# Adaptive-norm modulation moved from TensorE products to VectorE row sums, and the context's first norm moved into the feed-forward before it

## The chip, the cores and the metric

The kernel runs on one core of one Trainium2 chip. The metric is the device time of one execution in microseconds. Everything is fp32: products that need more than one pass of TensorE's reduced fp32 form are split by hand into a high and a low part (`whi`, `wlo` for weights, `Hhi`, `Hlo` for activations), the high part by a cast on ScalarE, the low part by a subtraction on VectorE.

## The reference, cut to what matters

256 tokens of 1024 features go through a first block (two layers: feed-forward, hybrid mixer, feed-forward) and a second block (two layers over the tokens and a context of 256 tokens). The second block is modulated by two condition vectors:

```python
def adaln(cond, w, b, n_chunks):
    return jnp.split(jax.nn.silu(cond) @ w + b, n_chunks, axis=-1)

# first block: per layer x += 0.5*ffn1(norm x); x += mixer(norm x); x += 0.5*ffn2(norm x); then a final norm
for layer in range(2):
    sh1, sc1, g1, sh2, sc2, g2 = adaln(c, w_mod[layer], b_mod[layer], 6)
    h_lat = rmsnorm(x, norm1_g[layer]) * (1 + sc1) + sh1
    if layer == 1:
        csh1, csc1 = adaln(c_ctx, w_mod[layer][:, :2 * D_MODEL], b_mod[layer][:2 * D_MODEL], 2)
    else:
        csh1, csc1, cg1, csh2, csc2, cg2 = adaln(c_ctx, w_mod[layer], b_mod[layer], 6)
    h_ctx = rmsnorm(ctx, norm1_g[layer]) * (1 + csc1) + csh1
    ...
```

`w_mod` is 2 x 1024 x 6144: 96 tiles of 512 KB. The result for one condition vector is 2 x 6144 numbers, 96 columns of 128 partitions (`MOD`, whose last index is 0 for c and 1 for c_ctx).

## The kernel before, in words

Each engine runs its own list of instructions, written out by hand; the order within an engine is the order of the code, and semaphores join the engines. The stages follow each other: for each layer l of the first block `("ffn1", l)`, `("in", l)` and `("out", l)` (the mixer), `("ffn2", l)`; then `c0` and `x0` (mixer of the second block's layer 0 on the context and on the tokens), `ffc` and `ffx` (its feed-forwards), `ctx_keys_values`, `x1`, and then the routed experts, which take the last 780 us and are not touched.

All weights but `w_mod` are one stream of 512 KB units through a ring of RAW = 11 buffers (`raw`), issued by SyncE. For a unit ScalarE writes `whi` (ring of SPLIT = 6), VectorE writes `wlo`, TensorE uses both and counts `weight_used`. `upto(n)` on ScalarE and VectorE stands for the casts up to unit n.

A feed-forward has NF = 22 steps f: a gate unit, an up unit and, two steps later, a down unit of 24 matmuls. On VectorE (`hidden`) a step is: wait for the gate unit, sum its halves into `gs`, one cast, the low part `hlo` of the step before, wait for the up unit, sum into `us`, multiply into `hd`, two casts. Behind the last step stand the residual adds (`ffn`). Small side jobs are put between: in both `ffn2` the 17 steps of the Hyena filter (`filter_step`; tables by GpSimd's `filter_tables`), in `ffn1` of layer 0 the turning of the context (`first_step`), in `ffc` and `ffx` the norm of the next stage's input (`side_step`).

A norm squares eight tiles (ScalarE), sums them over partitions with a matrix of ones (TensorE), takes sqrt (ScalarE) and reciprocal (VectorE), and then scales tile after tile: VectorE `TT`, ScalarE `HB` high, VectorE `HB` low.

The modulation has six groups of 16 tiles (three for each layer; a tile is 128 rows of `w_mod` by 1024 columns). SyncE loads them between weight units (`mods`) into up to 13 slots. `modulate` multiplies each with `CS`, silu of both condition vectors in 2 of 32 columns, on TensorE: 8 k by 4 column blocks, each a product of 512 columns. `rows_out` (ScalarE) copies the sums out of PSUM to `MR`, `turn_rows` (TensorE) transposes them, `take_rows` (VectorE) adds the bias into `MOD`. Groups 0, 1, 2 and 3 stand around norms (the first two k in front, the other six behind), group 4 in `ffc` at f = 13 and f = 20, group 5 in `ffx` at f = 13 and behind the norm in `ctx_keys_values`.

Behind `("ffn2", 1)` come the final norm of X, the scales `GS`, the norm of the context C with its modulation, and then c0's linear. GpSimd's `fold` adds eight tiles of squares to one, for norms that run beside other work; TensorE then needs one product only (`side_sum`).

## Time and profile before

| | |
|---|---|
| median of 3 runs | 3023.56 us (3022.86 to 3027.97) |
| the profiled execution | 3024.66 us, its span 3022.8 us |
| TensorE, VectorE, ScalarE, GpSimd busy | 2935.2, 2213.8, 1721.4, 75.3 us |
| instructions | 50779 |
| DMA | 692.13 MB, mean 229 GB/s |

Busy time of TensorE is near its span because matmuls are pipelined; where it waits is read from the chain of waits and from the idle time in brackets. In a timeline a row gives the start, the time, the engine, the line, the operation with its tiles, the number of instructions merged into it, and in brackets the idle time of the engine in front of it and what ended that. The tile names `M`, `scratch` and `gscratch` are shared buffers: `COND`, `gs`, `us` and `MR` lie in `M`.

### The profile page before, as it was taken

Reading aid. Unit: us, or ns where it says so; the run is one execution under the profiler, and the core shown is the slowest. Engines: PE = TensorE matmul, PEld = TensorE weight load, DVE = VectorE, ACT = ScalarE, POOL = GpSimd, SP = SyncE. Lnnn points to the kernel's source line nnn. Section 1 sums busy time; section 2 is a strip of 40 time slices with the busy share of each in tenths; the row PEclk is TensorE's granted clock in tenths of the full one; section 3 lists DMA queues with packets and bytes.
Section 4 is the critical chain, followed back from the end, with each engine's and each line's share of the span. In section 5 each row is a group of like instructions: output and inputs, shape, how many; then the busy total and the mean of one; then the engine's idle time right before and its main releaser. Section 6 shows DMA issues by size and latency. Waiting matters only on the chain.

```text
span 3022.8 us, 50779 instructions
## 1 busy us (share of the span) xinstructions
PE 2935.2 (97%) x18783; PEld 2569.6 (85%) x18783; DVE 2213.8 (73%) x2982; ACT 1721.4 (57%) x2379; POOL 75.3 (2%) x103
## 2 busy tenths in 40 slices
PE   9999999999999999999999999999989999999998
PEld 7989788899887889788889888997978888888887
DVE  6667666666677666566676767765678999999998
ACT  4446553444655445445544444455468788878886
POOL 2000000000000000000000000000000000000000
PEclk9999999999999999999999999999999999999999
DMA  8854465886536593465386775735559999999999
GB/s 253 274 181 140 128 189 182 259 274 186 161 119 177 161 282 102 140 175 162 86 253 186 223 238 180 230 105 151 174 197 362 364 354 362 367 361 359 364 363 335
DMA packets 664465, 692.13 MB, mean 229 GB/s; under 512 B 22830, under 2 KB 518145, under 8 KB 663008
## 3 DMA queue, kind: packets, MB, share of 16 engines
q1 hardware_dynamic: 658432, 665.06, 68.4%
q0 software_dynamic: 5712, 24.54, 2.2%
q8 instruction: 124, 2.03, 0.3%
q14 instruction: 53, 0.43, 0.0%
q10 hardware_dynamic: 144, 0.07, 0.0%
HBM read 684.86 MB, written 4.72 MB: 228 GB/s over the span
## 4 chain that ended last, share of the span: by engine, by line
PE 88%; DVE 6%; ACT 3%; issue 2%; DMA 1%; DVEq 0%; POOL 0%; ACTq 0%
PE W L694 35%; PE ACC L694 20%; PE W L787 15%; PE W L788 8%; PE W L687 4%; PE ACC L687 3%; DVE wlo L1885 1%; ACT whi L1393 1%; PE ACC L1001 1%; PE W L1211 1%; PE ACC L1202 0%; DVE R L1904 0%; DVE TT L1911 0%; DVE gs L1973 0%; DVE M L2038 0%
## 5 line engine op out<-in xcount | busy, mean ns | idle before, releaser
L1885 DVE TENSOR_TENSOR wlo<-raw,whi 128x1024 fp32r<-128x1024 f32 (+3 forms) x681 | 765.7, 1144 | 357.9 <-ACT whi L1393 355.8
L1393 ACT ACTIVATE whi<-raw 128x1024 fp32r<-128x1024 f32 (+3 forms) x681 | 655.6, 985 | 48.5 <-PE W L694 31.7
L2394 DVE TENSOR_TENSOR wlo<-raw,whi 128x1024 fp32r<-128x1024 f32 x528 | 617.7, 1221 | 43.3 <-ACT whi L1751 34.3
L787 PE MATMUL W<-HB,whi 128*128 128x512 f32 x1760 | 635.2, 403 | 12.6 <-DVE HB L1907 11.9
L1751 ACT ACTIVATE whi<-raw 128x1024 fp32r<-128x1024 f32 x528 | 547.5, 1060 | 94.7 <-PE W L694 52.7
L788 PE MATMUL W<-HB,wlo 128*128 128x256 f32 x1760 | 496.6, 282 | 0.0
L694 PE MATMUL W<-HB,whi 128*128 128x256 f32 x2592 | 480.2, 287 | 14.0 <-DVE HB L1907 8.1
L694 PE MATMUL W<-whi,HB 128*128 128x512 f32 (+1 forms) x1664 | 478.7, 373 | 4.9 <-issue 3.5
L694 PEld LDWEIGHTS W<-HB,whi 128*128 128x128 f32 x2592 | 407.4, 193 | 22.8 <-issue 12.7
L787 PEld LDWEIGHTS W<-HB,whi 128*128 128x128 f32 x1760 | 333.0, 189 | 102.7 <-issue 17.2
L1465 ACT ACTIVATE sg<-gs 128x256 f32<-128x256 f32 x132 | 55.1, 418 | 593.1 <-DVE gs L1973 593.1
L694 PE MATMUL W<-HB,wlo 128*128 128x256 f32 x1296 | 368.4, 284 | 0.0
L694 PEld LDWEIGHTS W<-whi,HB 128*128 128x128 f32 x1664 | 300.2, 189 | 60.3 <-DVE wlo L2394 4.4
L788 PEld LDWEIGHTS W<-HB,wlo 128*128 128x128 f32 x1760 | 335.6, 191 | 0.0
L694 PE MATMUL W<-wlo,HB 128*128 128x512 f32 (+1 forms) x832 | 307.8, 370 | 0.0
L694 PE MATMUL ACC<-hhi,whi 128*128 128x256 f32 x1056 | 303.9, 288 | 0.0
L694 PE MATMUL ACC<-hlo,whi 128*128 128x256 f32 x1056 | 298.9, 283 | 0.0
L694 PE MATMUL ACC<-hhi,wlo 128*128 128x256 f32 x1056 | 298.8, 283 | 0.0
L694 PEld LDWEIGHTS W<-HB,wlo 128*128 128x128 f32 x1296 | 250.6, 193 | 0.0
L1973 DVE TENSOR_REDUCE gs<-W 128x256 f32<-128x512 f32 x132 | 91.1, 690 | 164.1 <-PE W L788 164.0
L694 PEld LDWEIGHTS ACC<-hhi,whi 128*128 128x128 f32 x1056 | 200.6, 190 | 10.3 <-issue 4.8
L694 PEld LDWEIGHTS ACC<-hlo,whi 128*128 128x128 f32 x1056 | 200.8, 190 | 2.4 <-issue 2.4
(462 smaller groups left out, 4047.2 us busy)
## 6 DMA issues: line engine op xcount, KB each, us to landing
raw<-in_moe_w_gate SPq DMA_DIRECT2D x183, 512.0 KB, 5.3
raw<-in_moe_w_up SPq DMA_DIRECT2D x180, 512.0 KB, 5.4
raw<-in_ffn_w_in SPq DMA_DIRECT2D x176, 512.0 KB, 3.9
raw<-in_moe_w_down SPq DMA_DIRECT2D x176, 512.0 KB, 5.5
raw<-in_w_in SPq DMA_DIRECT2D x105, 512.0 KB, 4.8
raw<-in_ffn_w_out SPq DMA_DIRECT2D x88, 512.0 KB, 3.6
scratch<-in_w_mod SPq DMA_DIRECT2D x60, 512.0 KB, 7.3
raw<-in_mix_w_in SPq DMA_DIRECT2D x48, 512.0 KB, 3.7
```

The source lines that it names most:

```text
L687: return mm(o, a, b, start=start, stop=stop, skip_group_check=True)
L694: last = mm(o, a, b, start=start and i == 0, stop=stop and i == 2, skip_group_check=True)
L787: mm(o, wh[:, w], both(k), start=k == 0, stop=False, skip_group_check=True)
L788: last = mm(o[:, 0:T], wl[:, w], high[:, k, :], start=False, stop=k == KT - 1, skip_group_check=True)
L1001: last = nc.tensor.transpose(bank(4 + b % 2)[:, w], P2[:, (4 * i + b) % 3, w], ident[:, :])
L1211: last = nc.tensor.transpose(W[:, 2 * (g % 2), at], hdt[:, g % 2, at], ident[:, :])
L1393: A_(whi[:, g % SPLIT, 0:LONG[g]], raw[:, g % RAW, 0:LONG[g]], ACT.Copy).then_inc(weight_high, 1)
L1465: A_(sg[:, f % 2, 0:T], gs[:, f % 2, 0:T], ACT.Silu).then_inc(gated, 1)
L1751: A_(whi[:, g % SPLIT, :], raw[:, g % RAW, :], ACT.Copy).then_inc(weight_high, 1)
L1885: V.tensor_tensor(wlo[:, g % RAW, 0:LONG[g]], raw[:, g % RAW, 0:LONG[g]], whi[:, g % SPLIT, 0:LONG[g]].bitcast(F32), ALU.subtract).then_in ...
L1973: return V.tensor_reduce(o, W[:, b, :].rearrange("p (i t) -> p t i", i=2), AX.X, ALU.add)
L2394: V.tensor_tensor(wlo[:, g % RAW, :], raw[:, g % RAW, :], whi[:, g % SPLIT, :].bitcast(F32), ALU.subtract).then_inc(weight_split, 1)
```

## The change

The weights of the modulation come transposed from the host: row n of `w_mod_laid[l]` is column n of `w_mod[l]`, so a tile of 128 outputs by 1024 inputs is 512 KB in one piece. Both condition vectors are broadcast to all partitions (`COND`, silu on ScalarE). One instruction on VectorE multiplies a tile by a condition vector and writes the sum of each row into a column of `MOD`. There are 96 tiles; the first 64 are used for both vectors, the other 32 for c alone: 160 instructions. `MOD_STEPS` says at which step f of which feed-forward a tile is used: 18 in `("ffn1", 0)`, 7 in `("ffn2", 0)`, 22 in `("ffn1", 1)`, 6 in `("ffn2", 1)`, 21 in `ffc`, 22 in `ffx`; in both `ffn2` they stand at steps 2, 10, 12 and so on. GpSimd issues the loads (`mod_tiles`; three slots, one slot in both `ffn2`), and `condition` loads the vectors anew four times, since their buffer is used otherwise between. `modulate`, `turn_rows`, `rows_out`, `take_rows` and `mods` are gone.

The second part: the norm of C for c0 is made in `("ffn2", 1)`. ScalarE squares at f = 13 and 14, GpSimd folds, TensorE sums at f = 18, ScalarE takes sqrt at f = 19, VectorE scales tiles 0 to 3 at f = 20 and 21, the rest and the low parts behind the last step and in front of the residual adds. The final norm of X is now made in c0's linear: squares on ScalarE in front of it, a fold on GpSimd, one sum on TensorE in front of unit 4, sqrt at unit 4, reciprocal at unit 5 and the scaling of a tile in each of units 5 to 12.

The diff, cut to its core:

```diff
+        COND = M[:, 2048:4096].rearrange("p (i k) -> p i k", i=2)
+        JUNK = M[:, 5120:6144]
+
+        def mod_slot(name, i):
+
+            s = 0 if name in FILTERS else i % 3
+            if s == 0:
+                return s, M[:, 4096:5120]
+            return s, (G if name[0] == "ffn1" else S)[:, s * 1024:(s + 1) * 1024]
+
+        def mod_load(name, i):
+
+            u = MOD_FIRST[name] + i
+            return sum(mod_slot(n, j)[0] == mod_slot(name, i)[0] and MOD_FIRST[n] + j <= u
+                       for n in MOD_STEPS for j in range(len(MOD_STEPS[n])))
 
...
+        MOD_STEPS = {("ffn1", 0): range(4, 22), ("ffn2", 0): (2, 10, 12, 14, 16, 18, 20), ("ffn1", 1): range(0, 22),
+                     ("ffn2", 1): (2, 10, 12, 14, 16, 18), "ffc": range(1, 22), "ffx": range(0, 22)}
+        MOD_FIRST, at = {}, 0
+        for name, steps in MOD_STEPS.items():
+            MOD_FIRST[name] = at
+            at += len(steps)
+        assert at == 96
+        COND_AT = {("ffn1", 0): 3, ("ffn2", 0): 2, ("ffn2", 1): 2, "ffc": 1}
+        SIDE = {("ffn2", 1): 0, "x0": 1, "ffc": 2, "ffx": 3}
+        SIDE_INPUT = ("ffc", "ffx")
...
+            def keep_filter(l):
                 pool.wait_ge(freq_taken, 5 * l + 5)
                 pool.dma_start(kept[l], S[:, 2816:5376]).then_inc(kept_out, 16)
-
-            def fold(e, o):
-
-                pool.wait_ge(side_squares, KT * e + KT)
+                pool.wait_ge(kept_out, 16 * l + 16)
+
+            def condition():
+                for i, v in enumerate((A["c_2"][0], A["c_ctx_2"])):
+                    pool.dma_start(COND[:, i, :], v.partition_broadcast(128)).then_inc(cond_in, 16)
+
+            def mod_tiles(name, first, last):
+                for i in range(first, last):
+                    s, dst = mod_slot(name, i)
+                    u = MOD_FIRST[name] + i
+                    if i >= (1 if name in FILTERS else 3):
+                        pool.wait_ge(mod_used, u if name in FILTERS else u - 2)
+                    elif i == 0 and u:
+                        pool.wait_ge(mod_used, u)
+                    if name == ("ffn1", 1) and i == 1:
+                        pool.wait_ge(weight_used, start[name] + 1)
+                    pool.dma_start(dst, A["w_mod_laid"][u // 48, u % 48 * 128:u % 48 * 128 + 128, :]).then_inc(mod_landed[s], 16)
...
+                if l == 0:
+                    condition()
+                mod_tiles(("ffn1", l), 0, len(MOD_STEPS["ffn1", l]))
                 filter_tables(("ffn2", l), l)
+                condition()
+                mod_tiles(("ffn2", l), 0, 5)
+                if l == 1:
+                    fold(flat, side_squares, KT, side_folded)
+                mod_tiles(("ffn2", l), 5, len(MOD_STEPS["ffn2", l]))
+                keep_filter(l)
+            fold(flat, last_squared, KT, last_folded)
             for inst, l, full in MIXES:
...
-            def modulate(group, k0, k1, o):
-                for k in range(k0, k1):
-                    for c in range(2):
-                        u = 16 * group + 2 * k + c
-                        pe.wait_ge(mod_landed[u % 16 % ring(group)], 16 * mod_loads(u))
-                    for j in range(4):
-                        w = mod_slot(16 * group + 2 * k + j // 2)[:, j % 2 * 512:j % 2 * 512 + 512]
-                        last = f32(o[32 * j:32 * j + 32, :], CS[:, k, :], w, k == 0, k == KT - 1)
-                    last.then_inc(mod_used, 2)
...
+                    if name == ("ffn2", 1) and kind == "up" and f == 18:
+                        pe.wait_ge(freq_taken, 10)
+                        side_sum(SIDE[name], W[:, 3, 0:T])
...
-            modulate(3, 0, 2, W[:, 3, :])
-            norm()
-            modulate(3, 2, KT, W[:, 3, :])
+            pe.wait_ge(side_root, 1)
             mix2("c0")
...
+            def early_step(f):
+
+                if f in (13, 14):
+                    for k in range(4 * (f - 13), 4 * (f - 12)):
+                        A_(TT[:, k, :], C[:, k, :], ACT.Square).then_inc(side_squares, 1)
+                if f == 19:
+                    act.wait_ge(side_sums, 1)
+                    A_(R[:, :], W[:, 3, 0:T], ACT.Sqrt, bias=epsc, scale=1.0 / D).then_inc(side_root, 1)
 
...
+                    if COND_AT.get(name) == f:
+                        act.wait_ge(cond_in, 32 * list(COND_AT).index(name) + 32)
+                        A_(COND[:, :, :], COND[:, :, :], ACT.Silu).then_inc(cond_ready, 1)
...
+            def mod_part(name, f, i):
+
+                if f not in MOD_STEPS[name]:
+                    return
+                j = MOD_STEPS[name].index(f)
+                u = MOD_FIRST[name] + j
+                both = u < 64
+                if i == 0 and not both:
+                    return
+                s, w = mod_slot(name, j)
+                if i == 0 or not both:
+                    dve.wait_ge(mod_landed[s], 16 * mod_load(name, j))
+                    if u:
+                        dve.wait_ge(mod_used, u)
+                    if j == 0 and name in COND_AT:
+                        dve.wait_ge(cond_ready, list(COND_AT).index(name) + 1)
+                st = i if both else 0
+                ins = V.scalar_tensor_tensor(w if i else JUNK, w, 1.0, COND[:, st, :], ALU.mult, ALU.mult,
+                                             accum_out=MOD[:, u // 48, u % 48, st:st + 1])
+                if i == 1:
+                    ins.then_inc(mod_used, 1)
+
+            def add_bias(l, t0, t1, both):
+
+                n = 2 if both else 1
+                dve.wait_ge(mod_used, 48 * l + t1)
+                link(V.tensor_tensor(MOD[:, l, t0:t1, 0:n], MOD[:, l, t0:t1, 0:n],
+                                     PV[:, 2, 48 * l + t0:48 * l + t1].unsqueeze(2).broadcast_to([128, t1 - t0, n]), ALU.add))
 
             def first_step(f):
...
+            def early_step(f):
+
+                if f == 4:
+                    add_bias(0, 0, 48, True)
+                    for w in range(2):
+                        scales(0, w)
+                if f == 20:
+                    dve.wait_ge(side_root, 1)
+                    link(V.reciprocal(R[:, :], R[:, :]))
+                if f in (20, 21):
+                    for k in range(2 * (f - 20), 2 * (f - 19)):
+                        side_scale(0, k)
+
...
+                    if f < NF - 1:
+                        mod_part(name, f, 0)
                 low(NF - 1)
+                for i in range(2):
+                    mod_part(name, NF - 1, i)
+                if name == ("ffn2", 1):
+                    for k in range(4, KT):
+                        side_scale(SIDE[name], k)
+                    for k in range(KT):
+                        side_low(SIDE[name], k)
...
```

Three places in the order of instructions. VectorE, two steps' length of `("ffn1", 1)`, before (`gs` and `us` are the sums of the gate and the up unit, `wlo` the casts):

```order
L1885 TENSOR_TENSOR wlo<-raw,whi 128x1024 x2
L1973 TENSOR_REDUCE gs<-W 128x256
L1885 TENSOR_TENSOR wlo<-raw,whi 128x1024
L1977 TENSOR_TENSOR hlo<-hd,hhi 128x256
L1973 TENSOR_REDUCE us<-W 128x256
L2000 TENSOR_TENSOR hd<-sg,us 128x256
L1885 TENSOR_TENSOR wlo<-raw,whi 128x1024 x2
L1973 TENSOR_REDUCE gs<-W 128x256
```

The same place after; the form that writes `MOD` is the multiplication with row sums:

```order
L1893 TENSOR_TENSOR wlo<-raw,whi 128x1024 x2
L1947 SCALAR_TENSOR_TENSOR M,MOD<-gscratch,M 128x1024
L2021 TENSOR_REDUCE gs<-W 128x256
L1947 SCALAR_TENSOR_TENSOR gscratch,MOD<-gscratch,M 128x1024
L1893 TENSOR_TENSOR wlo<-raw,whi 128x1024
L2025 TENSOR_TENSOR hlo<-hd,hhi 128x256
L2021 TENSOR_REDUCE us<-W 128x256
L2049 TENSOR_TENSOR hd<-sg,us 128x256
L1893 TENSOR_TENSOR wlo<-raw,whi 128x1024 x2
L1947 SCALAR_TENSOR_TENSOR M,MOD<-gscratch,M 128x1024
```

One multiplication has moved in front of the gate sum and one behind it. VectorE at the end of `("ffn2", 1)` and the beginning of c0, before (`C` is the context, `X` the tokens; the last cast of c0's first units is at the end):

```order
L1977 TENSOR_TENSOR hlo<-hd,hhi 128x256
L1973 TENSOR_REDUCE us<-W 128x256
L2000 TENSOR_TENSOR hd<-sg,us 128x256
L1885 TENSOR_TENSOR wlo<-raw,whi 128x1024 x2
L1977 TENSOR_TENSOR hlo<-hd,hhi 128x256
L1885 TENSOR_TENSOR wlo<-raw,whi 128x1024
L2017 SCALAR_TENSOR_TENSOR X<-ACC,X 128x256 x8
L1885 TENSOR_TENSOR wlo<-raw,whi 128x1024
L1904 RECIPROCAL R<-R 128x256
L1911 SCALAR_TENSOR_TENSOR X<-X,PV,R 128x256 x8
L1871 MEMSET small 1x1
L2456 SCALAR_TENSOR_TENSOR GS<-MOD,PV 128x8 x2
```

And after:

```order
L2021 TENSOR_REDUCE us<-W 128x256
L2049 TENSOR_TENSOR hd<-sg,us 128x256
L1893 TENSOR_TENSOR wlo<-raw,whi 128x1024 x2
L2025 TENSOR_TENSOR hlo<-hd,hhi 128x256
L1982 SCALAR_TENSOR_TENSOR TT<-C,GS,R 128x256 x4
L1988 SCALAR_TENSOR_TENSOR HB<-TT,MOD,HB 128x256 x8
L1893 TENSOR_TENSOR wlo<-raw,whi 128x1024
L2075 SCALAR_TENSOR_TENSOR X<-ACC,X 128x256 x8
L1893 TENSOR_TENSOR wlo<-raw,whi 128x1024 x6
L2325 RECIPROCAL TT<-TT 128x256
L2327 SCALAR_TENSOR_TENSOR X<-X,PV,TT 128x256
```

The scaling of C and its low parts (`HB`) now stand in front of a cast and of the residual adds (`X<-ACC,X`); the norm of X is behind six casts. TensorE at the same place, before (the products with `CS` are the modulation, those with `ones` the norms):

```order
L694 MATMUL ACC<-hhi,wlo 128x256
L687 MATMUL W<-scratch,CS 32x512 x8
L687 MATMUL W<-TT,ones 128x256 x8
L687 MATMUL W<-scratch,CS 32x512 x4
L687 MATMUL W<-M,CS 32x512 x6
L687 MATMUL W<-gscratch,CS 32x512 x8
L687 MATMUL W<-scratch,CS 32x512 x6
L687 MATMUL W<-TT,ones 128x256 x8
L694 MATMUL W<-HB,whi 128x256 x2
L694 MATMUL W<-HB,wlo 128x256
```

After:

```order
L720 MATMUL ACC<-hhi,whi 128x256
L720 MATMUL ACC<-hlo,whi 128x256
L720 MATMUL ACC<-hhi,wlo 128x256
L720 MATMUL W<-HB,whi 128x256 x2
L720 MATMUL W<-HB,wlo 128x256
L720 MATMUL W<-HB,whi 128x256 x2
L720 MATMUL W<-HB,wlo 128x256
```

Between the last down unit (`ACC`) and c0's first unit (`W<-HB`) nothing is left.

## Rows read from the trace of the kernel before

**Rows 1.** Page, busy time of each engine and share of the span:

```profile
PE 2935.2 (97%) x18783; PEld 2569.6 (85%) x18783; DVE 2213.8 (73%) x2982; ACT 1721.4 (57%) x2379; POOL 75.3 (2%) x103
```

**Rows 2.** Page, chain of waits that ended last, by engine:

```profile
PE 88%; DVE 6%; ACT 3%; issue 2%; DMA 1%; DVEq 0%; POOL 0%; ACTq 0%
```

**Rows 3.** Groups of instructions by form, TensorE: count, busy us, mean ns, idle before:

```profile
L687 PE MATMUL W<-scratch,CS 128*32 128x512 f32 x240 | 32.9, 597 | 1.8 <-DMA scratch<-in_w_mod 1.8
```

**Rows 4.** Chain of waits in order of time: start us, us, what:

```profile
1121.68 5.52 PE W L687 x32
...
1134.26 3.73 PE W L687 x16
...
1150.94 0.44 PE ACC L750 x4
...
1687.67 3.57 PE W L687 x32
```

**Rows 5.** Timeline of VectorE in a step of ffn1, layer 1:

```profile
708.93 2.35 DVE L1885 TENSOR_TENSOR wlo<-raw,whi 128x1024 fp32r<-128x1024 f32 x2
712.79 0.69 DVE L1973 TENSOR_REDUCE gs<-W 128x256 f32<-128x512 f32 x1 [1.50 <-PE W L788]
714.91 1.23 DVE L1885 TENSOR_TENSOR wlo<-raw,whi 128x1024 fp32r<-128x1024 f32 x1 [1.43 <-ACT whi L1393]
```

**Rows 6.** Groups of instructions by form, VectorE:

```profile
L1907 DVE SCALAR_TENSOR_TENSOR HB<-TT,HB 128x256 fp32r<-128x256 f32 x48 | 20.1, 420 | 2.5 <-ACT HB L1423 2.5
L2044 DVE SCALAR_TENSOR_TENSOR scratch<-scratch 128x1536 f32<-128x1536 f32 x4 | 7.0, 1750 | 0.0
L2394 DVE TENSOR_TENSOR wlo<-raw,whi 128x1024 fp32r<-128x1024 f32 x528 | 617.7, 1221 | 43.3 <-ACT whi L1751 34.3
```

**Rows 7.** Timelines of VectorE, TensorE, ScalarE behind ffn1, layer 0:

```profile
210.34 2.91 DVE L2017 SCALAR_TENSOR_TENSOR X<-ACC,X 128x256 f32<-128x256 f32 x8 [0.82 <-PE ACC L694]
212.39 1.92 PE L687 MATMUL W<-scratch,CS 128*32 128x512 f32 x16
214.67 1.28 ACT L1417 ACT_TABLE_LOAD   x1
218.00 0.47 ACT L1417 ACTIVATE R<-W,small 128x256 f32<-128x256 f32 x1 [2.05 <-PE W L687]
```

**Rows 8.** Timelines of VectorE and ScalarE around the beginning of c0:

```profile
1117.19 0.42 DVE L1977 TENSOR_TENSOR hlo<-hd,hhi 128x256 fp32r<-128x256 f32 x1
1119.56 2.92 DVE L2017 SCALAR_TENSOR_TENSOR X<-ACC,X 128x256 f32<-128x256 f32 x8 [0.81 <-PE ACC L694]
1154.29 0.38 ACT L1652 ACTIVATE M<-W 128x256 f32<-128x256 f32 x1 [1.98 <-PE W L694]
```

**Rows 9.** Two norms: a window (TensorE busy, its load, VectorE, ScalarE, GpSimd, clock), timelines:

```profile
356.00:358.00 2.00, 0.70 (x2) 0.56 (x3) 1.82 (x6) 1.33 (x3) 0.00 (x0) 0.50 0.00 0
361.78 0.42 DVE L1907 SCALAR_TENSOR_TENSOR HB<-TT,HB 128x256 fp32r<-128x256 f32 x1 [0.24 <-ACT HB L1423]
365.84 0.69 DVE L1973 TENSOR_REDUCE us<-W 128x256 f32<-128x512 f32 x1 [1.28 <-PE W L788]
580.63 0.43 DVE L1907 SCALAR_TENSOR_TENSOR HB<-TT,HB 128x256 fp32r<-128x256 f32 x1 [0.24 <-ACT HB L1423]
584.54 0.69 DVE L1973 TENSOR_REDUCE us<-W 128x256 f32<-128x512 f32 x1 [0.65 <-PE W L788]
```

**Rows 10.** GpSimd's issue of a table, its landing, ScalarE behind it, a wide form:

```profile
368.01 0.60 POOL L634 DMA_DIRECT2D scratch<-in_k_dft  x1
379.34 0.42 ACT L1590 ACTIVATE scratch<-gscratch 64x256 f32<-64x256 f32 x1 [2.79 <-DVE gscratch L2148]
scratch<-in_k_dft POOLq DMA_DIRECT2D x5, 1408.0 KB, 10.0
L1659 ACT ACTIVATE TT<-M 128x1280 f32<-128x1280 f32 x3 | 3.8, 1273 | 0.6 <-ACTq L1382 0.4
```

**Rows 11.** Timeline of GpSimd, a fold in ffx:

```profile
1840.61 5.15 POOL L642 TENSOR_TENSOR TT<-TT 128x1024 f32<-128x1024 f32 x3 [190.76 <-ACT TT L1443]
```

More of the change, by code:

```diff
@@ L39 @@
 ITEMS = 2 * NE
+WARM = 18
 RAW = 11
@@ L695, in mm3, with linear @@
                 return last
-            def linear(p, units, x, to, by_tile=None, group=None, off=0, free=None, ahead=None, drain=True):
+            def linear(p, units, x, to, by_tile=None, off=0, free=None, ahead=None, drain=True):
                 N = len(units)
                 for n, (kt, nn) in enumerate(units):
-                    if group is not None and n == 2:
-                        turn_rows(group, ACC4[:, 0, :])
                     if ahead is not None:
@@ L763, in ffn @@
                         pe.wait_ge(dve_to_pe, heard.next("dve_to_pe"))
-                    if group is not None and n == 3:
-                        turn_rows(group, W[:, 3, :])
                     pe.wait_ge(weight_split, p + n + 1)
@@ L1801, in _ @@
                 ffn(("ffn2", l))
-            norm(X, after="tiles", ahead=start["c0in"] + AHEAD)
             mix2("c0", 0)
@@ L1941, in first_step, with scales @@
                     V.tensor_scalar(negR[:, :], mask[:, :], 1.0, 2.0 ** 100, ALU.subtract, ALU.mult)
[L1943 removed]
+            SIDES = ((C, 0, 1, 0, 0, Hhi, Hlo), (C, 24, 1, 0, 1, Ghi, Glo), (X, 24, 0, 0, 1, Hhi, Hlo),
+                     (C, 0, 1, 1, 0, Ghi, Glo))
+            def scales(l, w):
+                for st in range(1 if l and w else 2):
+                    V.scalar_tensor_tensor(GS[:, l, st, w, :], MOD[:, l, 8 + 24 * w:16 + 24 * w, st], 1.0,
+                                           PV[:, 3, 16 * w + 8 * l:16 * w + 8 * l + 8], ALU.add, ALU.mult)
+                settle()
             def side_scale(e, k):
@@ L2010, in summed, with ffn @@
                     dve.wait_ge(weight_used, start[name] + sizes[name])
-            def ffn(name, gate, res, group=None, tiles=True):
-                hidden(name, group)
+            def ffn(name, gate, res, tiles=True):
+                hidden(name)
                 for n in range(KT):
@@ L2452, in _ @@
                 ffn(("ffn2", l), lambda n: 0.5, X)
-            def scales(l, w):
-                for st in range(2):
-                    V.scalar_tensor_tensor(GS[:, l, st, w, :], MOD[:, l, 8 + 24 * w:16 + 24 * w, st], 1.0,
-                                           PV[:, 3, 16 * w + 8 * l:16 * w + 8 * l + 8], ALU.add, ALU.mult)
-                settle()
-            norm(X, lambda k: PV[:, 3, 74 + k:75 + k], to=X, told=True, ahead=start["c0in"] + AHEAD)
-            for w in range(2):
-                scales(0, w)
             mix2("c0", 0)
```

223 lines of the change are left out of this document (93 added, 130 removed).

## The prediction

> **What bounds the kernel now.** I read the busy shares first [rows 1]: TensorE is busy for 97% of the span, VectorE for 73%. Then the chain of waits [rows 2]: 88% of it is TensorE's own work. So anything taken off TensorE's queue in a stretch where it never waits is worth its full length, and anything put on VectorE is free only while it fits into that engine's own idle time. Then I asked for the groups of instructions [rows 3]: the modulation's products are 384 matmul records (one of its three groups of rows is shown; 192 products, two records each), with a stationary operand of 32 columns. Last the chain in order of time, at each place where they stand [rows 4].
>
> **Part A, products inside ffc and ffx.** There the chain of waits holds three blocks of 32 records with 3.57 us each [rows 4] (one is shown, the others begin at 1751 and 1883 us). TensorE runs without a pause around them, so they go in full: 3 x 3.57 = 10.7 us. The fourth such block stands behind the norm in front of x1, where TensorE waits for VectorE's normalised tiles anyway: 0.
>
> **Part B, the turns.** Six groups of four transposes; one takes 0.44 us [rows 4]. The one in c0 is counted in part D; five are left, 5 x 0.44 = 2.2 us.
>
> **Part C, products around three norms** (ffn1 to mix of both layers, ffn2 of layer 0 to ffn1 of layer 1). The first two k of a group stand in front of the norm's matmuls and take 1.9 us [rows 7]; the other six stand behind them, where TensorE waits for sqrt, reciprocal and tiles, and cost nothing. What is late next: ScalarE's table load ends at 215.95 (214.67 + 1.28) and its sqrt starts at 218.00, so 2.05 us are to be had there [rows 7]. Behind ffn2 of layer 0 nothing new stands at the end of the steps: 1.9 us. Behind both ffn1, VectorE has two new multiplications before its last cast and the residual adds. The adds, which began at 210.34 after a pause, begin some 1.6 us later, the squares and the table load move with them, and only some 0.5 us of the 2.05 is left. Against it, TensorE now idles where the products stood, and its clock falls: in front of ffn2 of layer 0, a norm without products, it is granted 0.50 (the 1.2 GHz level), and from the last tile (361.78) to the sum of the second unit (365.84) are 4.06 us; in front of ffn1 of layer 1, with products, it is 3.91 us (580.63 to 584.54) [rows 9]. That is 0.15 us, three times 0.5. Part C: 1.9 + 0.5 + 0.5 - 0.5 = 2.4 us.
>
> **Part D, the context's first norm.** Before, the last down unit of ffn2 ends at 1121.68, where the norm's 32 records start [rows 4]; then come X's norm, C's squares and norm (1134.26), the scaling, and c0's third unit ends at 1154.29, where ScalarE is released [rows 8]: 32.6 us. After, the scaled context is ready when ffn2 ends. VectorE's last hlo starts at 1117.19; four scalings (0.40 each), eight low parts (0.40) and one cast (1.2) end at about 1123.5; TensorE needs tile k at 1121.7 + 0.36k, and the last low part is done at about 1122.3, in time for the eighth tile. So three units of 24 matmuls (2.88 each) end 8.6 us after ffn2: 24.0 us less. Added on TensorE: one sum in ffn2 and one in c0, 0.43 each (half of a two-tile stretch at 0.22 a record). Residual adds move from 1119.56 [rows 8] to 1123.5, X's squares end at 1127, GpSimd's fold takes 5.15 us [rows 11] and ends at about 1132.1; TensorE reaches its sum in front of unit 4 at 1133.2. ScalarE's cast for unit 4 is done at about 1128. The cover is 1 us for the fold and 4 us for the cast. Part D: 24.0 - 0.9 = 23.1 us.
>
> **Part E, what VectorE gets.** 160 multiplications over 128x1024. The trace has none with a row sum. Nearest rows [rows 6]: a scalar_tensor_tensor over 256 columns takes 420 ns, over 1536 columns from SBUF 1750 ns, a tensor_tensor over 1024 columns 1221 ns. They lie on one line (about 150 ns + 1.04 ns a column), so 1.22 us without the sum; with it I take 1.3. The bounds are 1.22 and two passes over the tile, 150 + 2 x 1070 = 2.29 us. In a step of ffn1 VectorE has two pauses: 1.50 us before the gate sum, released by TensorE, and 1.43 us before the next cast, released by ScalarE [rows 5]. The order shows one multiplication at each place. At 1.3 both fit, by 0.2 and 0.1 us, so the 40 steps with a pair in ffn1 and the 11 in ffc cost 0; steps of ffx have one. At 1.47 they still fit on the average; beyond, each step is late by twice the excess. The Trainium skill (VectorE: DVE Perf Modes, "Two Vector instructions with no wait between them") says that an operation with an accumulator output is two instructions, the second a read of the accumulator. No row here shows one; that rule would make the 1.22 somewhat longer, as in my 1.3.
>
> **Part F, new waits for transfers.** In each ffn2 ScalarE now waits at f = 2, behind its sine, for c and c_ctx (1 MB), which GpSimd's queue issues right behind the table k_dft. That table is issued at 368.01 and takes 10.0 us for 1408 KB [rows 10]; 1024 KB more at that rate land at about 385. ScalarE is there at 379.7; the silu over 2048 columns takes some 2.0 us (1273 ns for 1280 columns [rows 10]). Behind the waiting ScalarE stand two casts, then VectorE's casts, its multiplication and the next gate sum; casts run 387 instead of 380. TensorE has about four units (11 us) of split weights left, so the first burst is just covered; the next step has 4.5 us of filter work on ScalarE (abs, table load, two exp) and there I count 2 us of pause. Two such places: -4 us, with bounds 0 (all covered) and -16 (both casts of two steps late in full). In ffn1 of layer 0 and in ffc the same silu stands at f = 3 and f = 1 beside idle ScalarE: 0. Weight tiles of the modulation were 96 x 512 KB before and are as many now, only from GpSimd's queue: 0.
>
> **Sum.** 10.7 + 2.2 + 2.4 + 23.1 + 0 - 4 = 34.4 us. The profiled execution took 3024.66 (span 3022.8 and 1.9 around it), 1.1 above the median of 3023.56. 3024.66 - 34.4 = 2990.3, and 2989.2 by the median; I say 2989.
>
> **Rivals.**
> R1, slower: the row sum makes the multiplication take two passes. Place: VectorE's queue in both ffn1. It decides from 1.47 us on. At 2.29 a pair costs 4.58 against 2.93 of pauses, 1.65 a step; 40 steps are 66 us, which show in full because the residual adds stand behind them in the same queue. In ffc 11 x 1.65 = 18, of which later steps with one multiplication give back 6 and TensorE's lead covers some: 10. 2989 + 76 = 3065. Against it: the rows without a sum run at one column a beat whether inputs come from SBUF or not [rows 6]. The Trainium skill (Vector Engine (DVE) Microarchitecture Reference, "Points that are easy to get wrong") says that this form with two sources in SBUF that aren't bf16 halves its throughput, with no port left for the accumulator's readback. By that rule the 1536-column row would be near 3.3 us if it held for every such instruction; it is 1.75, so without a sum the trace contradicts it, and with one no row decides.
> R2: the hand-over to c0 is late, since VectorE's queue at the end of ffn2 (scalings, low parts, cast, adds) slips by 3 us and the fold behind it too: TensorE waits for tiles and again before unit 4, some 12 us of the 23 go. 3001. For it: the fold's cover is only 1 us. Against: the cast has 4.
> R3: the transfers of part F land 7 us later than worked out (the DMA engines are full there): 8 us at each ffn2 instead of 2, 3001 as well, up to 3005 with the start of ffc.
>
> **How the numbers follow.** Forecast 0.70 (own range 2983 to 2996), R1 0.12, R2 0.09, R3 0.07, and 0.02 that parts cancel. The range of 8 in 10 takes in R2 and R3 and part of what a multiplication at 1.5 would add: 2981 to 3008. Within 0.2% means 3017.5 to 3029.6, about what a measurement of this kernel can tell from no change; only the last case and a mild R1 (1.8 us) lie there: 0.03. Slower: 0.10. Faster: 0.87.
>
> **What would show it.** Right: row sums at 1.25 to 1.45 us; the pauses of VectorE in ffn1 shrunk to 0.1 to 0.3 with the steps' period unchanged; no block of 3.57 in ffc and ffx; c0's first unit directly behind ffn2's last, at full clock; in norms behind ffn1 a granted 0.50. Wrong: a multiplication of over 1.5 us with TensorE waiting for wlo or hlo in ffn1 (R1); TensorE idle before c0's first or fifth unit (R2); TensorE waiting for wlo at f = 4 or 5 of ffn2, behind a ScalarE that waits for a DMA (R3).

## The result, and the profile after

The changed kernel takes 3005.38 us (median of 4 runs, 3001.36 to 3006.27), beside 3023.21 for the kernel before on the same chip: a ratio of 0.9936, with a 95% interval of 0.9923 to 0.9948. It is faster, inside the wide range of 2981 to 3008 but outside the forecast's own, 2983 to 2996: it gains 18 us where 34 were forecast. The profiled run took 3005.84 (span 3004.0).

The busy shares of the changed kernel, and its chain of waits by engine [rows 1, 2]:

```profile
PE 2899.5 (97%) x18347; PEld 2564.1 (85%) x18347; DVE 2399.1 (80%) x3295; ACT 1724.6 (57%) x2377; POOL 144.8 (5%) x213
PE 81%; DVE 8%; ACT 4%; issue 3%; DMA 2%; SPq 1%; POOL 0%; POOLq 0%; DVEq 0%; ACTq 0%
```

TensorE is busy for 35.7 us less. VectorE has 185 us more. But TensorE's part of the chain fell from 88% to 81%: new waits came in, through VectorE, ScalarE and, new in such a size, DMA.

What TensorE waited for from 20 to 1200 us (us in total, times, longest; four rows of the list):

```profile
PE W L791 <- DVE HB L1915: 11.9, 3, 4.0
PE W L720 <- DVE HB L1915: 9.4, 2, 4.7
PE W L713 <- DVE gscratch L2217: 6.4, 2, 3.5
PE W L828 <- ACT C L1496: 3.9, 3, 3.4
```

The first two are the norms' tiles, five waits of 21.3 us in all. The kernel before had three of 11.9, one of them in c0; its products stood at three of the five. The third and the fourth are new and were in no term of the sum: the filter's damping in both ffn2 (L2217), and a copy of the context in ffn1 of layer 0 (3.4 us once; all such waits were 0.7 us before).

I set the two traces against each other at TensorE's first matmul of each block. Rows of after, from the timeline of TensorE:

```profile
50.72 0.94 PE L828 MATMUL W<-ident,scratch 128*128 128x128 f32 x4 [3.42 <-ACT C L1496]
225.38 0.76 PE L720 MATMUL W<-HB,whi 128*128 128x256 f32 x2 [4.67 <-DVE HB L1915]
358.90 0.76 PE L791 MATMUL W<-HB,whi 128*128 128x512 f32 x1 [3.97 <-DVE HB L1915]
421.72 1.09 PE L713 MATMUL W<-gscratch,scratch 64*128 64x512 f32 x2 [2.88 <-DVE gscratch L2217]
582.06 0.47 PE L791 MATMUL W<-HB,whi 128*128 128x512 f32 x1 [3.97 <-DVE HB L1915]
781.08 0.54 PE L720 MATMUL W<-HB,whi 128*128 128x256 f32 x2 [4.73 <-DVE HB L1915]
916.04 0.77 PE L791 MATMUL W<-HB,whi 128*128 128x512 f32 x1 [3.97 <-DVE HB L1915]
979.54 1.19 PE L713 MATMUL W<-gscratch,scratch 64*128 64x512 f32 x1 [3.55 <-DVE gscratch L2217]
1147.62 0.70 PE L713 MATMUL ACC<-TT,ones 128*128 128x256 f32 x2 [0.73 <-POOL TT L652]
```

The same places in both kernels (the last down matmul of a block or the first of the next; from x0's norm on, the named operation of VectorE), and what each stretch lost or gained:

| stretch, to the mark | before | after | change in the stretch |
|---|---|---|---|
| start to the end of ffn1, layer 0 | 212.18 | 216.45 | +4.3 |
| norm and mix, to ffn2 | 357.30 | 358.90 | -2.7 |
| ffn2, layer 0 | 566.39 | 574.35 | +6.4 |
| norm, ffn1 of layer 1 | 766.57 | 772.14 | -2.4 |
| norm and mix, to ffn2 | 910.05 | 916.04 | +0.4 |
| ffn2, layer 1 | 1121.68 | 1135.21 | +7.5 |
| to the end of c0's third unit | 1154.29 | 1143.85 | -24.0 |
| to x0's norm (reciprocal) | 1349.84 | 1341.03 | +1.6 |
| to x0's last residual add | 1574.80 | 1565.75 | -0.2 |
| ffc | 1769.94 | 1753.92 | -7.0 |
| ffx | 1962.16 | 1941.95 | -4.2 |
| to the last add of x1 | 2204.03 | 2182.93 | -0.9 |
| routed part, to the end | 3022.8 | 3004.0 | +2.3 |

The end of c0's third unit is worked out after, as 1135.21 + 3 x 2.88 us, since nothing stands between. The column adds up to -18.8 us. The losses of note are 4.3, 6.4 and 7.5 us, in the first 1140 us. The 2.3 us of the routed part are scatter: it is the same code in every kernel here and takes 818.5 to 821.2 us in the eleven traces.

**Ffn2, layer 0.** ScalarE around the condition's silu (start, us, what), and TensorE's clock after its pause (a window; the granted clock is the third figure from the end):

```profile
384.23 1.92 ACT L1479 ACTIVATE M<-M 128x2048 f32<-128x2048 f32 x1 [2.50 <-DMA M<-in_c_ctx]
386.05 1.99 ACT L1393 ACTIVATE whi<-raw 128x1024 fp32r<-128x1024 f32 x2
424.00:426.00 2.00, 2.00 (x9) 1.71 (x8) 0.90 (x1) 0.00 (x0) 0.00 (x0) 0.50 0.00 0
```

The transfers had landed at 384.2 (forecast 385), and the casts run at 386.05 (forecast 387). Nothing stopped there: TensorE lived on its stock. It stopped 33 us later, at the second of the filter's four products for the taps, which waits for VectorE's damping of the first (418.84 to 421.72), and after 2.88 us of pause its clock was 0.50 (the 1.2 GHz level) for some more. The wait is in one place and the cause in another, four steps of the block earlier. On VectorE the casts behind ScalarE's silu and the damping, after:

```profile
387.12 2.36 DVE L1893 TENSOR_TENSOR wlo<-raw,whi 128x1024 fp32r<-128x1024 f32 x2 [4.79 <-ACT whi L1393]
420.89 0.68 DVE L2217 TENSOR_TENSOR gscratch<-W,TT 128x512 f32<-128x512 f32 x1
```

And the same two before, when the block began 1.6 us earlier:

```profile
380.74 2.36 DVE L1885 TENSOR_TENSOR wlo<-raw,whi 128x1024 fp32r<-128x1024 f32 x2 [0.38 <-ACT whi L1393]
414.81 0.69 DVE L2161 TENSOR_TENSOR gscratch<-W,TT 128x512 f32<-128x512 f32 x1
```

Counted from the block's start the casts are 4.8 us late and the damping is still 4.5 us late.

Another part of the loss lies 40 us further on, at a pause of 0.88 us that both kernels have. Behind it the clock falls in the changed kernel and not in the one before (first the changed kernel's pause and a window behind it, then a window of before behind its pause at 455.62):

```profile
461.96 1.05 PE L713 MATMUL W<-ones,TT 128*128 128x1 f32 x8 [0.88 <-DVE TT L2226]
464.00:466.00 2.00, 2.00 (x8) 1.72 (x7) 2.00 (x3) 0.00 (x0) 0.00 (x0) 0.50 0.11 32
```

```profile
457.00:459.00 2.00, 2.00 (x14) 1.75 (x13) 1.89 (x2) 0.00 (x0) 0.00 (x0) 1.00 0.42 125
```

From windows of 2 us, each of the two falls in layer 0 costs 1.7 us, so the 6.4 us are about 2.9 of pause, 1.7 of clock behind it and 1.7 of clock behind the pause of 0.88. In layer 1 they are 3.55, 3.4 and 1.7, and 0.43 for the new sum; a wait of 2.08 us for a small table of the filter, which the kernel before had, is gone.

**The start.** The longest piece of the chain, a weight tile on its way for 22.83 us, ScalarE's wait for weights, and the first issue of the condition:

```profile
17.47 22.83 DMA raw<-in_ffn_w_out
39.01 1.06 ACT L1393 ACTIVATE whi<-raw 128x1024 fp32r<-128x1024 f32 x1 [3.06 <-DMA raw<-in_ffn_w_in]
23.04 0.58 POOL L634 DMA_DIRECT2D M<-in_c  x1
```

The condition and three tiles (2.5 MB) are issued from 23.04 on, beside the weights, and weights come late: ScalarE's longest wait for them between 26 and 50 us was 0.36 us before.

**The multiplication with a row sum** [rows 6], the largest of its groups, and VectorE in a step of ffn1, layer 1 [rows 5]:

```profile
L1947 DVE SCALAR_TENSOR_TENSOR M<-M 128x1024 f32<-128x1024 f32 x73 | 89.3, 1224 | 0.0
701.31 0.69 DVE L2021 TENSOR_REDUCE gs<-W 128x256 f32<-128x512 f32 x1 [0.35 <-PE W L792]
701.92 1.21 DVE L1947 SCALAR_TENSOR_TENSOR gscratch<-gscratch,M 128x1024 f32<-128x1024 f32 x1
703.06 0.08 DVE L1947 DVE_READ_ACCUMULATOR gscratch<-gscratch,M 128x1 f32 x1
703.44 1.23 DVE L1893 TENSOR_TENSOR wlo<-raw,whi 128x1024 fp32r<-128x1024 f32 x1 [0.30 <-ACT whi L1393]
```

1.22 + 0.08 = 1.30 us, as taken. The pauses shrank from 1.50 and 1.43 to 0.35 and 0.30, and the step still takes 8.53 us (701.31 to 709.85).

**The beginning of c0** [rows 4, 8]: the last down matmul of ffn2 and c0's first unit, then VectorE's residual adds and GpSimd's fold:

```profile
1135.09 0.28 PE L720 MATMUL ACC<-hhi,wlo 128*128 128x256 f32 x1
1135.21 0.40 PE L720 MATMUL W<-HB,whi 128*128 128x256 f32 x2
1137.92 2.73 DVE L2075 SCALAR_TENSOR_TENSOR X<-ACC,X 128x256 f32<-128x256 f32 x8
1141.26 2.41 POOL L652 TENSOR_TENSOR TT<-TT 128x1024 f32<-128x1024 f32 x1 [49.06 <-ACT TT L1660]
```

No gap between the two matmuls. The cover of the fold, worked out as 1 us, was 0.7 us short: the squares ended 5.9 us behind ffn2 in place of 5.3, and the fold took 6.3 us (1141.26 to 1147.58) in place of 5.15.

### The profile page after: what moved, and what is told of

It reads as the page before. It is cut to its first block, busy times and chain, and to the rows that moved or that the text cites. A ratio compares the mean times of both kernels' runs of the same rounds, so it can differ in the third digit from the quotient of the medians.

```text
span 3004.0 us, 50282 instructions
## 1 busy us (share of the span) xinstructions
PE 2899.5 (97%) x18347; PEld 2564.1 (85%) x18347; DVE 2399.1 (80%) x3295; ACT 1724.6 (57%) x2377; POOL 144.8 (5%) x213
## 4 chain that ended last, share of the span: by engine, by line
PE 81%; DVE 8%; ACT 4%; issue 3%; DMA 2%; SPq 1%; POOL 0%; POOLq 0%; DVEq 0%; ACTq 0%
PE W L720 34%; PE ACC L720 18%; PE W L791 14%; PE W L792 7%; PE ACC L713 3%; PE W L713 3%; DVE wlo L1893 3%; ACT whi L1393 2%; DMA M<-in_c_ctx 1%; DMA raw<-in_ffn_w_out 1%; PE ACC L1003 1%; PE W L1216 1%; DVE gs L2021 1%; SPq L543 1%; PE ACC L1207 0%
## 5 line engine op out<-in xcount | busy, mean ns | idle before, releaser
L791 PE MATMUL W<-HB,whi 128*128 128x512 f32 x1760 | 644.3, 408 | 16.6 <-DVE HB L1915 15.9
L792 PEld LDWEIGHTS W<-HB,wlo 128*128 128x128 f32 x1760 | 341.1, 194 | 0.0
L720 PEld LDWEIGHTS W<-HB,wlo 128*128 128x128 f32 x1296 | 252.1, 194 | 0.0
L720 PEld LDWEIGHTS ACC<-hhi,wlo 128*128 128x128 f32 x1056 | 202.0, 191 | 0.0
```

The lines of the kernel that those rows point to most:

```text
L720: last = mm(o, a, b, start=start and i == 0, stop=stop and i == 2, skip_group_check=True)
L791: mm(o, wh[:, w], both(k), start=k == 0, stop=False, skip_group_check=True)
L792: last = mm(o[:, 0:T], wl[:, w], high[:, k, :], start=False, stop=k == KT - 1, skip_group_check=True)
```

## The experiments

All are edits of the changed kernel; their diffs are cut to the core. Ratios are to the kernel before, run on the same chip beside them, with their 95% intervals; the changed kernel's own is 0.9936 [0.9923, 0.9948].

**1. The condition late in both ffn2.**

```diff
-("ffn2", 0): (2, 10, 12, 14, 16, 18, 20)      ("ffn2", 1): (2, 10, 12, 14, 16, 18)
+("ffn2", 0): (10, 11, 12, 14, 16, 18, 20)     ("ffn2", 1): (10, 11, 12, 14, 16, 18)
-COND_AT = {..., ("ffn2", 0): 2, ("ffn2", 1): 2, "ffc": 1}
+COND_AT = {..., ("ffn2", 0): 10, ("ffn2", 1): 10, "ffc": 1}
-                if f == 4:      # early_step: bias and gains of layer 0
+                if f == 11:
```

> The changed kernel with, in both ffn2, the silu of the condition on ScalarE and the first pair of multiplications moved from step 2 to step 10 (steps 10, 11, 12, 14, 16, 18, and 20 in layer 0). All transfers stay where they are. Theory A (ScalarE's wait, its silu and VectorE's first pair at step 2 push both queues back, the damping of the filter's taps comes late, TensorE waits 2.88 and 3.55 us for it and then runs at the 1.2 GHz level for some us): the 6.4 us lost in ffn2 of layer 0 and the 7.5 us lost in layer 1 come back but for about 1 us, so 3005.4 - 13 = 2992, and no wait of TensorE for gscratch of over 1 us. Rival B (it is the transfers: 1.5 MB more right behind k_dft hold the weights up): the issues are unchanged, so 3005 and the two waits stay.

Measured: 2997.87 us, 0.9911 [0.9896, 0.9926]. TensorE's marks in the trace:

```profile
360.06 0.77 PE L791 MATMUL W<-HB,whi 128*128 128x512 f32 x1 [3.97 <-DVE HB L1915]
577.41 0.47 PE L791 MATMUL W<-HB,whi 128*128 128x512 f32 x1 [3.97 <-DVE HB L1915]
910.29 0.77 PE L791 MATMUL W<-HB,whi 128*128 128x512 f32 x1 [3.97 <-DVE HB L1915]
1134.63 0.70 PE L713 MATMUL ACC<-TT,ones 128*128 128x256 f32 x2 [0.74 <-POOL TT L652]
```

Both waits for the damping are gone. Ffn2 of layer 0 with the norm behind it takes 217.35 us instead of 223.16, and from ffn2 of layer 1 to the sum in c0 it is 224.34 instead of 231.58: 5.8 + 7.2 = 13.0, as expected. c, c_ctx and the first tile are issued behind k_dft as before, so rival B is out; only the second tile, which waits for the first one's use, comes later, and run 9 leaves that one in its place. The median gives back only 7.5 of the 13; where the rest is, comes behind the fourth run.

**2. Only VectorE's pair late.** As 1, with COND_AT left at 2.

> As the run before it, but only VectorE's first pair of multiplications moves to step 10; ScalarE still waits for c and c_ctx at step 2 and does the silu there. Theory A, with ScalarE's part (2.5 us of wait and 1.9 of silu) the larger: VectorE's queue is relieved of 2.6 us at step 2, TensorE's waits for the damped taps shrink from 2.9 and 3.6 to about 0.5 and 1, so some 7 us come back, 2998. Rival C (the pair on VectorE is all that matters): the same time as the run before it, 2992. Rival B: 3005.

Measured: 3001.53 us, 0.9924 [0.9911, 0.9938]. The two waits are still there, smaller:

```profile
422.96 1.09 PE L713 MATMUL W<-gscratch,scratch 64*128 64x512 f32 x2 [1.35 <-DVE gscratch L2217]
975.49 1.09 PE L713 MATMUL W<-gscratch,scratch 64*128 64x512 f32 x2 [1.12 <-DVE gscratch L2217]
```

By the same marks 3.2 and 4.8 us come back, though the median gives back only 3.9 of the 7 expected. So the pair is a part of the cause and not all of it: rival C falls. In layer 0 this trace has no fall of the clock behind the pause of 1.35 us, but it has the one behind the pause of 0.88 us.

**3. The first transfers held back.**

```diff
+                    pool.wait_ge(weight_used, start["ffn1", 0] + 8)
                     condition()
-COND_AT = {("ffn1", 0): 3, ...
+COND_AT = {("ffn1", 0): 4, ...
```

> The changed kernel with the first issue of c, c_ctx and three weight tiles held back in GpSimd's queue until TensorE has used eight units of ffn1, layer 0 (about 45 us instead of 23), and the silu at step 4 instead of 3. Theory A (2.5 MB at 23 us, where the DMA engines are full with weights, tables and context, cost ffn1 of layer 0 its stock of weights: +4.3 us at its end, with TensorE waiting 3.4 us at 50.7): the 4 us come back, 3001, and the wait of 3.4 us is gone. Rival D (the pairs on VectorE make this block longer, not the transfers): 3005. Rival E (the later silu, on a ScalarE that now waits at step 4, costs as much): 3005 with a wait at 55 to 60 us.

Measured: 2999.80 us, 0.9917 [0.9903, 0.9930]. The pause at 50.7 and the next norm:

```profile
47.33 0.63 PE L829 MATMUL W<-ident,scratch 128*128 128x128 f32 x4 [0.84 <-ACT C L1497]
220.46 0.76 PE L721 MATMUL W<-HB,whi 128*128 128x256 f32 x2 [4.67 <-DVE HB L1916]
```

At the second row the kernel is 4.9 us ahead of the changed one (225.38). The six traces with the changed kernel's start and its pairs reach this row at 225.19 to 226.69, the three with the later start (runs 3, 4 and 8) at 220.46 to 221.25, so the gain is clear of that scatter. The pairs of multiplications are all there, so rival D doesn't explain it, and the later silu cost nothing that shows (E). The longest transfer in the chain still takes 15.68 us here, so not all of the 22.83 us came from the early issues.

**4. Both.** The edits of 1 and 3.

> The edits of the first and the third run together. Theory A: the gains add up, 3005.4 - 13 - 4 = 2988, which is the time forecast for the changed kernel (2989). Rival B or D: 3001 or more.

Measured: 2993.88 us (2989.37 to 2995.75), 0.9900 [0.9885, 0.9915]. The gains add up to the sum in c0: 1129.31 instead of 1147.62, 18.3 us. The profiled run took 2989.4, near the 2988 expected; the median is 4.5 us more. In these traces the same instructions differ by the clock. In the mix of x1 TensorE pauses 1.6 us for ScalarE in every kernel; windows from there, in the changed kernel (2045.85) and in this one (2028.52):

```profile
2045.85:2049.85 4.00, 3.99 (x24) 2.29 (x24) 2.20 (x5) 2.94 (x9) 0.00 (x0) 1.00 1.10 324
```

```profile
2028.52:2032.52 4.00, 3.98 (x17) 2.08 (x17) 2.21 (x5) 1.95 (x6) 0.00 (x0) 0.69 1.07 315
```

From x0's norm to the last norm of x1 the trace of the changed kernel, with no such fall, takes 845.9 us; those of runs 1 to 4 take 848.0 to 848.7. So the changed kernel's trace gained 2 to 3 us there that are not its own, though its whole time is no lower than its median, since its routed part took 2.3 to 2.6 us more than that of runs 2 to 4. The marks up to c0 measure the edits better than the total does. That this is where the rest of run 1's 13 us went is read from single traces, not shown: whether x1 is slower in most executions of run 1 than of the changed kernel is open.

**5. Row sums over 8 columns** in ffn1, ffc and ffx.

```diff
-                ins = V.scalar_tensor_tensor(w if i else JUNK, w, 1.0, COND[:, st, :], ...
+                ins = V.scalar_tensor_tensor((w if i else JUNK)[:, 0:c], w[:, 0:c], 1.0, COND[:, st, 0:c], ...
```

(c is 8 in these four blocks, 1024 elsewhere: this kernel leaves most of the modulation out.)

> The changed kernel with the row sums of ffn1 of both layers, of ffc and of ffx taken over 8 of the 1024 columns only (that part of the modulation is left out); waits, transfers and the row sums in ffn2 stay. Theory A (a multiplication of 1.22 + 0.08 us lies in VectorE's pauses, part E costs nothing inside the steps, and only the pair behind the last step of both ffn1 stands in front of the residual adds): the kernel gains at most 2 us, 3003 to 3005. Rival F (VectorE, with 0.35 and 0.30 us of pause left in a step, already slows the steps): 10 us or more are gained, under 2995.

Measured: 3002.68 us, 0.9932 [0.9915, 0.9949]. The interval doesn't part it from the changed kernel, and it excludes the 10 us of rival F. From ffn1 of layer 1 to the mix it is 1.5 us shorter (197.5 against 199.0 us); 0.7 of these are the shorter wait in the norm, 3.98 instead of 4.73. Behind ffn1 of layer 0 it is 2.1 us ahead (223.28 against 225.38), again 0.7 of it in the norm; the rest is within the scatter of that mark.

**6. One operation more in each step of ffn1, layer 1.**

```diff
+                if name == ("ffn1", 1) and i == 1:
+                    V.tensor_reduce(small[:, 60:61], w, AX.X, ALU.add)
```

> The changed kernel with one more operation of about the same length (a sum over 128x1024, some 1.2 us) on VectorE beside each pair in the 22 steps of ffn1, layer 1. Theory A (0.65 us of pause are left in a step of 8.53 us, so the step becomes bound by VectorE): 0.6 us a step, 13 us in all, less some 2 for the lead of TensorE: 3016 to 3019, with VectorE without a pause and TensorE waiting for wlo or hlo. Rival G (the pauses understate what VectorE can take, since its queue is only held in step by the others): under 3 us, 3005 to 3008.

Measured: 3014.47 us (3007.57 to 3017.57), 0.9961 [0.9950, 0.9971]. Its gate sums, with what stands between them, on VectorE, and TensorE at the end of the block:

```profile
700.79 0.69 DVE L2023 TENSOR_REDUCE gs<-W 128x256 f32<-128x512 f32 x1
701.40 1.21 DVE L1948 TENSOR_REDUCE small<-M 128x1 f32<-128x1024 f32 x1
709.61 0.69 DVE L2023 TENSOR_REDUCE gs<-W 128x256 f32<-128x512 f32 x1
775.89 0.55 PE L720 MATMUL ACC<-hhi,whi 128*128 128x256 f32 x1 [5.70 <-DVE hlo L2027]
```

VectorE has no pause left, and the step is 8.82 us instead of 8.53: 0.29, half of what was expected, since operations in a row start 0.08 us before the one ahead ends (1.21 us long, 1.13 apart). From the block's first matmul to the next mix it takes 208.9 instead of 199.0 us. 22 times 0.29 are only 6.4 of these 9.9 us; the first steps, which had no pause to begin with, grew by over 1 us each (6.56 to 7.69), and at the block's end TensorE pauses for the 5.70 us shown. Theory A holds in kind, its price was a quarter too high; G is out. So the changed kernel's ffn1 is within 0.8 us a step (0.35 + 0.30 + twice 0.08) of being bound by VectorE.

**7. X's sum of squares in front of c0's first unit.**

```diff
-                    if inst == "c0" and n == 4:
+                    if inst == "c0" and n == 0:
                         pe.wait_ge(last_folded, 1)
```

> The changed kernel with the sum of squares of X, and with it the wait for GpSimd's fold, in front of c0's first unit instead of its fifth. It prices the cover that four units of c0 give the residual adds, the squares and the fold. Theory A (the fold ends at 1147.5, TensorE is there at 1135.2): TensorE waits 12.3 us in place of 0.7 and then starts at half clock, so 12 to 15 us slower than the changed kernel, 3017 to 3020, so nearly half of part D's 24 us hangs on the order within c0. Rival H (c0's first units would wait for low parts of the context or for weights anyway): under 4 us, at most 3009.

Measured: 3019.33 us, 0.9985 [0.9975, 0.9994].

```profile
1144.12 1.19 PE L713 MATMUL ACC<-TT,ones 128*128 128x256 f32 x2 [11.44 <-POOL TT L652]
```

14 us slower than the changed kernel, and 13.3 us by the traces, from the end of ffn2 to x0's norm: without the four units in front of it, the wait for GpSimd's fold eats more than half of part D.

**8. What the runs point to.** The edits of 4, with these steps:

```diff
+("ffn2", 0): (12, 13, 14, 15, 16, 18, 20)     ("ffn2", 1): (12, 13, 14, 15, 16, 18)
+COND_AT = {("ffn1", 0): 4, ("ffn2", 0): 12, ("ffn2", 1): 12, "ffc": 1}
+                if f == 15:     # bias and gains of layer 0
+                mod_tiles(("ffn2", l), 0, 4)    # and then the fold
+                    if inst == "c0" and n == 5:     # X's sum; its sqrt, reciprocal and gain one unit later too
```

> The kernel of the fourth run (condition late in both ffn2, first transfers held back) with the silu and the first pair at step 12 (steps 12, 13, 14, 15, 16, 18, and 20 in layer 0), the bias and the gains at step 15, GpSimd's fold one tile earlier, and X's sum of squares in front of c0's sixth unit instead of its fifth. Theory A: the wait of 1.5 us for the filter's table at 1035 us goes, since the pairs no longer meet the two wide operations of step 11, and the 0.7 us before unit 4 go: 2 us below the fourth run, 2992. Rival: what is left is the clock and the spread of the routed part, and the time is the fourth run's, 2994.

Measured: 2986.67 us (2985.87 to 2989.31), 0.9878 [0.9861, 0.9894]: better than both kernels, 37 us below the first and some 18 below the changed one. Of TensorE's waits from 20 to 1200 us, the one that the new steps were for (the damping and the fold aren't in the list any more):

```profile
PE W L714 <- ACT scratch L1613: 2.6, 8, 0.9
```

The longest wait for ScalarE's scratch fell from 1.6 us in run 4 to 0.9, where it was expected to go. By the trace the new steps and the later sum are worth 2.1 us up to x0's norm (1322.05 against 1324.18). That the median is 7 us below run 4 is not theirs alone: this trace, like the changed kernel's, has no fall of the clock behind the pause of 1.6 us in x1.

**9. The condition in front of the filter's tables.**

```diff
+                pool.wait_ge(weight_used, start["ffn2", l] + 1)
+                condition()
                 filter_tables(("ffn2", l), l)
-                condition()
```

> The changed kernel with c and c_ctx of both ffn2 issued in front of the filter's tables instead of behind them, so that they have landed when ScalarE comes to them; the silu and the first pair stay at step 2. It parts the wait from the work. Theory A (of the 7 us by which VectorE's queue is late, 2.5 are ScalarE's wait for c_ctx, 1.9 its silu, 2.6 the pair): the wait goes, the work stays, TensorE's waits for the damped taps shrink by about 2.5 us, from 2.9 and 3.6 to some 0.5 and 1, 5 us in all: 3000. Rival J (only the transfer matters): as with all of it moved, 2997, with no such wait. Rival K (the filter's small tables and k_dft now land behind 1 MB, and TensorE or ScalarE waits for these instead): no gain, 3005 or more, with a wait at the filter's first product or in front of the exps.

Measured: 2998.02 us, 0.9912 [0.9898, 0.9925]. ScalarE's silu in layer 0, now without a wait, and TensorE's waits for a table and for the damping in layer 1 (in layer 0, 0.25 us of wait for the damping is left):

```profile
384.35 1.90 ACT L1480 ACTIVATE M<-M 128x2048 f32<-128x2048 f32 x1
927.34 0.64 PE L714 MATMUL W<-scratch 17*64 17x256 f32 x2 [1.48 <-DMA scratch<-in_hy_w]
973.71 1.09 PE L714 MATMUL W<-gscratch,scratch 64*128 64x512 f32 x2 [0.89 <-DVE gscratch L2218]
```

The waits left are those of A (0.5 and 1 us), the time is J's: the median gives back as much as with everything moved. By the marks 5.3 us come back in layer 0 and 5.9 in layer 1, 11.2 of run 1's 13.0. The small tables are waited for, 1.48 us in layer 1, where the changed kernel has no such wait and the kernel before had 2.08 us; K is right about that and wrong about the size.

## Why the prediction came out as it did

**Part D, right.** c0's third unit ends 24.0 us earlier against ffn2's end, as worked out. The sum in c0 and its wait took 1.6 back in place of 0.43: 0.43 of work, 0.73 of wait (the fold's cover was said to be 1 us), the rest a slower restart and what no row here names. With the other sum, in ffn2, 21.9 for 23.1. Rival R2 happened only in its small part, the 0.73 us of wait; run 7 shows what its kind can cost, 14 us for the 12 it named.

**Parts A and B, right.** No block of products is left in ffc and ffx: 7.0 + 4.2 + 0.9 = 12.1 for 12.9.

**Part C, too low.** Ffn2 to ffn1: 2.4 for 1.9. The two norms behind ffn1 show -2.7 and +0.4, but the mix behind them takes 30.7 or 32.1 us in traces of either kernel, by the clock after a pause of 2.36 us; it was the longer one before in layer 0 and after in layer 1. Without this 1.4 they gain 1.3 and 1.0 each, where 0.5 was said. That the products in front of the norm stood in the way of more than ScalarE's sqrt, as this says, was not tested by itself.

**Part E, right.** 1.30 us as taken, and from the fifth step on the period is that of run 5, whose sums are short, 8.53 us; run 5 finds no cost inside the steps, run 6 finds the edge close behind. In the first steps of ffn1, layer 1, 6.56 us long, VectorE already has no pause. Rival R1 needed 1.47. The Trainium skill's sentence behind it (Vector Engine (DVE) Microarchitecture Reference, "Points that are easy to get wrong"), read as the prediction reads it, does not hold for this operation: 1024 fp32 columns from SBUF take 1.22 us with a row sum, as long as the tensor_tensor of 1024 columns without one [rows 6]. The trace agrees with the Trainium skill's other rule (VectorE: DVE Perf Modes, "Two Vector instructions with no wait between them"): the accumulator's read is an instruction of its own, 0.08 us.

**Part F, the step that failed.** It said 4 us for both ffn2 and 0 for the start; the traces say 6.4 + 7.5, less the new sum of 0.43, and 4.3. Its arithmetic of the transfers and of ScalarE was right to 1 us. Wrong was "TensorE has about four units (11 us) of split weights left, so the first burst is just covered" with "there I count 2 us of pause".

I looked for the end of the cover in the weights of the next two steps. But the filter's chain (product, damping on VectorE, product) lies in the same queues and has no stock at all: the next of its products waits for the damping's place in VectorE's queue. ScalarE's wait (2.5 us), the silu (1.9) and the pair (2.6) fell into one step, 7.0 us in sum. The pair was in no term: part E prices the 40 pairs of ffn1 and the 11 of ffc, not the 13 of both ffn2. Against run 1, counted from the block's first matmul, VectorE's next gate sum is 5.0 us late and the damping four steps on still 4.2; the steps between gave back only 0.8.

Runs 1, 2 and 9 show it: to take away the pair gives 7.9 us, to take away the wait gives 11.2, to take away all of it 13.0. They don't add, since a delay costs only what goes beyond the cover. What goes beyond it cost about twice its length: 2.88 us of pause stand in 6.4 of loss, 3.55 in 7.5. Of the rest, 1.7 and 3.4 us are the clock right behind the pause. Another part is the clock's fall behind the pause of 0.88 us some 40 us on, which in layer 0 shows in all six traces with the silu at step 2 behind the tables (the changed kernel, runs 2, 3, 5, 6, 7) and in none of the other five, but in layer 1 is missing in runs 3 and 6 of those six. Why it comes there is open; so 1.7 us in each block can't be called the price of the delay for certain.

Rival R3 had the size (8 us at each ffn2, 3001 to 3005) by a wrong cause: it wanted the transfers 7 us later, and they landed on time. It also had the wrong sign to look for, TensorE waiting for wlo at f = 4 or 5.

**The start.** "In ffn1 of layer 0 ... beside idle ScalarE: 0" looked at the engine that does the silu and not at the transfers that feed it. "Weight tiles ... only from GpSimd's queue: 0" counted their bytes and not their time: before, they started behind 31 units of weights, at 82 us; now 2.5 MB start at 23 us. None of the rows taken from the kernel before is of these 50 us. Run 3 gives 4.9 us back by moving them.

Put right, with 13.5 in place of 4 for the ffn2 and 4.3 for the start, the sum would have been 34.4 - 9.5 - 4.3 = 20.6 us, beside 18.8 in the traces, of which 2.3 are the routed part's scatter.

That the measured time lies inside the range of 2981 to 3008 is in part luck: its upper end was set for R2, R3 and a longer multiplication, and what took the 16 us was none of them.

## What to carry to other kernels

When work moves into a queue that is said to have room, find the dependent chain with the least stock that runs through that queue, and follow the delay to it, even four steps on; the place to put the work is behind that chain. Add up all that a step receives (a wait, the operation behind it, the pair on the next engine) before asking what covers it. And a prefetch costs by when it starts: ask what is in flight at that time.
